# Shift products and head sums between the tiles of a weight chunk instead of in one block

## The reference

```python
# first network, per layer: queries and keys are normed per head of 64 columns
def rms_norm(x, g):
    y = x * lax.rsqrt(jnp.mean(x * x, axis=-1, keepdims=True) + EPS)
    return y * g

# second network: a norm with a scale and a shift made from the conditioning vector
m_l = (silu_c @ w_mod[i] + b_mod[i])[:, None, :]
sh1, sc1, g1, sh2, sc2, g2 = jnp.split(m_l, N_MOD, axis=-1)
hl = modulate(x, norm1_g[i], sh1, sc1)
x = x + g2 * sq_relu_mlp(modulate(x, norm2_g[i], sh2, sc2), mlp_w1[i], mlp_w2[i])
```

## Time and profile before

| | |
|---|---|
| device time, median of 3 runs | 3154.97 us (3154.85 to 3159.22) |
| span of the profiled execution, first to last instruction | 3151.0 us |
| what lies around the span, median less span | 4.0 us |
| TensorE busy (matmuls) | 3119.5 us, 14806 matmuls |
| VectorE, ScalarE, GpSimd busy | 1976.3, 1227.9, 614.9 us |
| DMA | 342.38 MB, mean 109 GB/s |

### The profile page before, as it was taken

The page is one execution under the profiler, slowest core; times in us unless marked ns, Lnnn a source line. Parts: engine busy times, 40 slices in busy tenths (PEclk is TensorE's granted clock), DMA queues, the critical chain, the costliest instruction groups (busy, mean ns, idle before and its releaser), DMA issues.

```text
span 3151.0 us, 36166 instructions
## 1 busy us (share of the span) xinstructions
PE 3119.5 (99%) x14806; PEld 2539.2 (81%) x14806; DVE 1976.3 (63%) x2658; ACT 1227.9 (39%) x1653; POOL 614.9 (20%) x479
## 2 busy tenths in 40 slices
PE   9999999999999999999999999999999999999998
PEld 7877788888888778888888766788888888888887
DVE  7555656566666467567766667766555589964333
ACT  4234443333432334422235356643333353342222
POOL 1000010000200010599981010002433101010001
PEclk9999999999999999999999999999999999999999
DMA  3222243455222222355533010023333422222221
GB/s 129 82 94 81 80 152 136 156 205 187 94 85 87 80 90 92 120 183 187 206 135 114 26 30 28 18 98 118 117 127 110 151 97 91 109 93 94 104 97 67
DMA packets 55620, 342.38 MB, mean 109 GB/s; under 512 B 5984, under 2 KB 7840, under 8 KB 18208
## 3 DMA queue, kind: packets, MB, share of 16 engines
q1 hardware_dynamic: 54080, 337.46, 30.0%
q10 hardware_dynamic: 1376, 2.62, 0.2%
HBM read 327.47 MB, written 12.58 MB: 108 GB/s over the span
## 4 chain that ended last, share of the span: by engine, by line
PE 79%; POOL 10%; DVE 6%; ACT 2%; issue 1%; DMA 0%; DVEq 0%; ACTq 0%; POOLq 0%
PE PS L264 78%; POOL FA L273 10%; ACT PB L270 1%; PE PS L267 1%; DVE FA L281 1%; DVE wl L273 1%; DVE PB L273 1%; DVE UL L273 1%; DVE PS L273 1%; DVE SC L273 1%; ACT SC L270 0%; DVE FA L273 0%; DVE ST L293 0%; ACT FA L270 0%; DMA CO<-in_consts 0%
## 5 line engine op out<-in xcount | busy, mean ns | idle before, releaser
L264 PE MATMUL PS<-UH,wh 128*128 128x512 f32 (+1 forms) x2120 | 835.7, 394 | 2.6 <-DVE UL L281 1.3
L264 PE MATMUL PS<-UL,wh 128*128 128x512 f32 (+1 forms) x2120 | 823.8, 389 | 0.0
L264 PE MATMUL PS<-UH,wl 128*128 128x512 f32 (+1 forms) x2120 | 823.7, 389 | 0.0
L273 DVE TENSOR_TENSOR wl<-raw,wh 128x2048 fp32r<-128x2048 f32 (+2 forms) x255 | 562.7, 2208 | 390.6 <-ACT wh L270 390.5
L264 PE MATMUL PS<-RH,wh 128*128 128x512 f32 (+2 forms) x1640 | 644.6, 393 | 0.4 <-DVE wl L273 0.4
L264 PE MATMUL PS<-RH,wl 128*128 128x512 f32 (+2 forms) x1640 | 639.4, 390 | 0.0
L264 PE MATMUL PS<-RL,wh 128*128 128x512 f32 (+2 forms) x1640 | 639.1, 390 | 0.0
L270 ACT ACTIVATE wh<-raw 128x2048 fp32r<-128x2048 f32 (+2 forms) x255 | 452.9, 1780 | 245.2 <-DMA raw<-in_wall 178.2
L264 PEld LDWEIGHTS PS<-UH,wh 128*128 128x128 f32 x2120 | 399.5, 188 | 103.5 <-issue 18.4
L264 PEld LDWEIGHTS PS<-UL,wh 128*128 128x128 f32 x2120 | 399.9, 189 | 83.6 <-issue 3.8
L264 PEld LDWEIGHTS PS<-UH,wl 128*128 128x128 f32 x2120 | 399.8, 189 | 82.7
(11 more groups left out here) (218 smaller groups left out, 3077.9 us busy)
## 6 DMA issues: line engine op xcount, KB each, us to landing
raw<-in_wall SPq DMA_DIRECT2D x224, 1024.0 KB, 4.8
FA<-in_wmod SPq DMA_DIRECT2D x48, 1024.0 KB, 4.9
raw<-in_wall SPq DMA_DIRECT2D x29, 512.0 KB, 3.6
kspec<-FA SPq DMA_DIRECT2D x8, 1024.0 KB, 7.0
FA<-kspec SPq DMA_DIRECT2D x8, 1024.0 KB, 6.8
PB<-in_window SPq DMA_DIRECT2D x16, 256.0 KB, 5.0
Hs<-in_xT ACTq DMA_DIRECT2D x4, 512.0 KB, 8.1
FA<-in_w SPq DMA_DIRECT2D x4, 512.0 KB, 5.7
```

Of the source, the lines that this page charges most:

```text
L264: return self.put(self.eng and self.eng.matmul(out, w, x, start=start, stop=stop, skip_group_check=True))
L273: return self.put(self.eng and self.eng.tensor_tensor(out, a, b, op))
```

## The change

In `first_x` the shift products no longer stand ahead of the chunk. The bank is taken and the shift waited for at the same place, but the four products of tile k (two m, high and low weights) are issued right behind that tile's six matmuls, and ahead of the square sums where those stand. The sum's signal comes with the last tile. Since both output columns now share one accumulation that begins once, only the very first product starts the bank. On VectorE `shift_sums(n)` moves from ahead of `norm(n)` to behind it.

In `layer`, only head sum 0 stays between chunk 2 and chunk 3. Sums 1, 2 and 3 stand behind the tiles t = 1, 3 and 5 of chunk 3's first output tile, sums 4 and 5 behind that output tile and sum 6 behind the second, as before.

```diff
@@ first_x @@
             p.wait_ge("w_lo", tag)
             if n in SHIFTED:
-                shift_products(tag, n)
+                take(("ws", n), ("ws", n))
+                p.wait_ge("gain", n)
             for key, fr in zip(keys, frees):
                 take(key, *fr)
...
                 if k < 7 and n in SHIFTED:
                     p.then_inc("early", (n, k))
+                if n in SHIFTED:
+                    shift_products(tag, n, k)
                 if n and k == SUMS_AT[n]:
                     square_sums(n)
...
-        def shift_products(tag, n):
-
-            take(("ws", n), ("ws", n))
-            p.wait_ge("gain", n)
+        def shift_products(tag, n, k):
+
             for m in range(2):
-                for k in range(8):
-                    for i, w in enumerate(pair(tag, 256 * k + 128 * m)):
-                        p.matmul(ps(("ws", n), 2, o=2 * m), w, SH[:, k, :], k == 0 and i == 0, k == 7 and i == 1)
-            p.then_inc("sum", ("ws", n))
+                for i, w in enumerate(pair(tag, 256 * k + 128 * m)):
+                    p.matmul(ps(("ws", n), 2, o=2 * m), w, SH[:, k, :], k == 0 and m == 0 and i == 0, k == 7 and i == 1)
+            if k == 7:
+                p.then_inc("sum", ("ws", n))
@@ layer @@
-                    for x in range(4):
-                        head_sum(l, x)
+                    head_sum(l, 0)
                     continue
                 for m, k in enumerate(ks):
                     key = ("qk", l, k)
                     take(key, ("qk_x", (l, k)))
-                    group(key, ps(key), [(pair(("qk", l, i), 256 * t + 128 * m), U(t), u_made(n, t)) for t in range(8)])
-                    for x in ((0, 1), (2, 3), (4, 5), (6,))[k - 4]:
+                    for t in range(8):
+                        three(ps(key), pair(("qk", l, i), 256 * t + 128 * m), U(t), t == 0, t == 7)
+                        if t == 7:
+                            p.then_inc("sum", key)
+                        elif m == 0 and t % 2:
+                            head_sum(l, 1 + t // 2)
+                    for x in ((4, 5), (6,))[m]:
                         head_sum(l, x)
@@ vector_program, the same at 8 and 9 @@
         w_lo(("up", 2, 0, 0))
+        norm(7)
         shift_sums(7)
-        norm(7)
         mlp(2, 7)
```

More of the change, by code:

```diff
@@ L2937, in vector_program @@
         w_lo(("up", 2, 0, 0))
+        norm(7)
         shift_sums(7)
-        norm(7)
         mlp(2, 7)
         w_lo(("hw", 0))
+        norm(8)
         shift_sums(8)
-        norm(8)
         hyena()
         w_lo(("up", 3, 0, 0))
+        norm(9)
         shift_sums(9)
-        norm(9)
         mlp(3, 9)
```

## The result

The changed kernel takes 3163.57 us in the median of 7 runs (3163.1 to 3169.44), the kernel before 3154.97 (7 runs, 3151.55 to 3159.51): a ratio of 1.0032, 95% interval 1.0022 to 1.0042. The change makes the kernel slower by 0.3%, above the 3161 at which the predicted range ended.

A forecast was written before the change was run, and what follows sets the result against it. TensorE was taken to bound the kernel, busy 3119.5 of 3151.0 us. Norms -6.2, layer 1 -1.2 and layer 0 +9.5 summed to +2.1 us, a forecast of 3157 us, range 3148 to 3161.

The forecast's parts named there:

- the one on `shift_sums`: Norms: VectorE's shift sum moved behind the norm costs nothing; if its cover failed, two instructions of 0.15 us would show.
- rival 3: Clock falls inside the norms' mixtures: +9.6 us a norm, 3168 us for one, over 3180 for all; chance 0.08.
- The norms: Norms 7, 8 and 9: clock no longer falls, -3.2, -1.5 and -1.5, together -6.2 us.
- The worry about the square sums: Norms: square sums behind tile 1 may wait for GpSimd's last addition; taken as 0.1 us (0 to 0.2).
- The uncovered part: Layer 0: TensorE stands still 3.0 us before its matmul at 54.26; 2.9 us of small products come uncovered.
- the forecast: Layer 0's clock rises only once the mixture is over, +9.5 us there; 3157 us in all, chance 0.45.
- rival 1: Clock rises inside layer 0's mixture: +3.7 there, including a 0.8 stall; 3151.3 us in all, chance 0.32.
- Layer 1: Head sums between tiles: clock -1.7, extra runs +0.1, stall 0.4; together -1.2 us.
- the 0.4: Layer 1: TensorE stalls 0.4 us (0 to 0.8) for the pooling chunk's low part, after late query roots.
- rival 2: Layer 0's clock never falls, or the norms gave away more than the trace shows: about 3148 us, chance 0.08.
- Rival 4: Clock falls have another cause and return beside the mixtures; only layer 0's 2.9 and stalls remain: 3159 us, chance 0.05.
- Rival 5: Small products' weights load behind the tiles, each followed at 0.02 not 0.11: 10.9 us less, 3146 us, chance 0.02.

The follow-up runs named there:

- the norms alone: Changed kernel with any PSUM bank allowed for Hyena's second weight chunk and head sums back in one block in both layers: 3147.75 us, ratio 0.9983.
- the blocks of sixteen: The earlier weights kernel with each norm's shift products in two blocks of sixteen, behind tiles 3 and 7, not eight of four: 3149.11 us, ratio 0.9983.
- the free bank: Changed kernel with Hyena's second weight chunk allowed any PSUM bank, not only the lower four: 3152.23 us, ratio 0.9998.
- the copy inside the norm: Changed kernel with VectorE's copy of norm 8's shift sum meant between the norm's tiles 4 and 5, not behind tile 7: 3157.68 us, ratio 1.0016.
- the copy ahead of it: Changed kernel with VectorE's copy of norm 8's shift sum ahead of the norm's first tile: 3158.42 us, ratio 1.0017.
- the head sums alone: Kernel before with only the change's head-sum part, in both layers, norms as before: 3158.93 us, ratio 1.0015.
- the earlier weights: The free bank kernel with ScalarE's first query-key high part in layer 0 allowed three places ahead, not one: 3146.27 us, ratio 0.9977.

## Why the prediction was wrong

**The step that failed** is the one on `shift_sums`: "Its readers (the bias of the first ReLU, the first Hyena tiles) stand behind that on VectorE anyway, so it costs nothing; if that cover failed, its two instructions of 0.15 us would show." It asked who reads the sum. The copy also hands back the bank, and TensorE's next taker of that bank was never looked for. It cost 8.2 us of waiting and 2.6 us of clock, 10.8 in the trace, where I had 0 and at worst 0.3; freeing the bank took 11.3 us off the median. With those 10.8 us the changed kernel is slower, without them it is not. That the two tiles of the second Hyena chunk start together, and that this chunk may use only four banks of eight, made it bite at norm 8 alone. The Trainium skill, "PSUM — Partial Sum Buffer", "PSUM bank collisions raise a hardware error", says to guard PSUM with semaphores by bank and quadrant of partitions, not by address. The trace shows what that means for time: four columns of a bank kept a product of 512 columns from starting for 8.20 us. No rival named this either; rival 3, the slower one, put its price on the clock inside the norms' mixtures, where it stayed at 1.00.

**The norms.** Predicted -6.2, measured -5.3 by the medians and -6.2 at the norms themselves in the trace (the norms alone). The clock is 1.00 at all three, so the cause named, the block of 32, was right. That the size fits is in part luck: it was taken from one execution, and norms 7 and 8 lost 3.4 or 6.8 us in different profiles, so a price read from one is uncertain by 1.7 us a place. The worry about the square sums proved sound: the products of two tiles cover exactly the 0.9 us by which GpSimd's addition would be late (shown by the blocks of sixteen).

**Layer 0.** The uncovered part was right: idle 3.05 us for the 3.0 forecast, 2.55 us in the short outcome for 2.9. Of the clock I had asked which of two ways it would go, 0.45 for the forecast and 0.32 for rival 1. Both happen in kernels that share this layer 0, by the groups in about half the executions each: the lower group has four of the changed kernel's 7 runs, and six of 11 with the free bank, with the copy inside the norm and with the copy ahead of it. All four profiles fit: low for 3.4 us in the one of a lower group, for 13.65 in the three of upper groups. The fifth kernel with it, the head sums alone, fits less well: its runs have no clear gap from 3156.5 to 3162.2, and the profiled one, low for 13.65 us, is at 3158.42, below the median. So the shares are a reading of the groups, not a count. The long way costs 6.8 us, not 9.5: my sum kept the low level to the end of the mixture, 68.06, and added half a stretch behind it, but the clock rose at 66.2. Rival 1's stall of 0.8 did not come either.

**Layer 1.** -1.4 in the trace for -1.2 predicted; in the medians nothing. VectorE's roots wait as worked out:

```profile
907.09 0.19 DVE L278 TENSOR_SCALAR RQ<-PS 128x32 f32<-128x32 f32 x1 [6.93 <-PE PS L264]
```

They are 6.9 us later than in the earlier trace rows, 4.3 when the 2.6 by which the whole kernel runs late there are taken off, for the 4.0 of the prediction. No stall follows; the 0.4 was not needed.

**The sum.** Without the bank's price it is -0.5 or -0.8, 3152 to 3154.5 us, inside the range and below the 3157 forecast, mostly for layer 0's clock. With it, 3163.6 falls outside.

**Rivals 2, 4, 5.** Low stretches do come and go (rival 2), but places elsewhere take them up. Rival 4 falls, since the blocks' low stretches are gone. Rival 5 falls too: the products at 2511.11 to 2511.36 are 0.03, 0.11 and 0.11 apart. The Trainium skill's rule on pulled-ahead weight loads ("TensorE: Matmul & The Clock Gate", "What happens when you issue a matmul") holds for one product of a run, as it did in the earlier trace rows.

Left open: what decides between layer 0's two outcomes in one execution, and why some profiles have the low stretches at 901, at 1722 and 1790 or at the end and others not.

## What to carry to other kernels

When an instruction that empties a buffer is moved later, look for two parties: who reads the result, and who takes the buffer next; the second is found only by following the hand-out of banks, and a restriction to a few banks brings it close. Breaking up long blocks of tiny matmuls was worth 5.3 us at the three norms, where nothing behind them was late, and nothing that the medians show in layer 1. Where the block is cover, first bring forward what TensorE waits for. When pricing a stretch of low clock, halve only the time in which TensorE is busy. A profile shows one execution: low-clock stretches that are 3.4 us long and cost 1.7 should be priced from several, and times be read as groups before medians are compared.

## What the runs showed of the hardware

The same layer 0 came out of a wait of 3.05 us into a mixture of large and small matmuls with 3.4 us at 1.2 GHz (one profile) or with 13.65 (four), which took 9.70 and 13.99 us from its first large matmul to the key sums. With 0.47 us of waiting in front, the same mixture kept 2.4 GHz in both profiles taken (the earlier weights, and the blocks of sixteen). Sixteen two-column matmuls in a row (1.8 us) were followed by no low stretch at three norms of one profile. 32 in a row (3.5 us) were followed by one at all three norms in three profiles and in layer 0 in five, but in layer 1 in only two of four. Eight small records take 0.95 us at the upper level and 1.70 at the lower, so they pay the clock almost in full even though they stream two columns.
